# Mixer and MLP of a transformer block project x times the norm's weights, and multiply by the norm's root when the result leaves PSUM

## The reference

```python
x = x + 0.5 * gate * swiglu(h, w2_gu, w2_down)      # end of the first block (not shown: where h comes from)
x = rms_norm(x, g_final)                            # the first block's output

def second_block(x, mem, ...):
    x = x + token_mixer(rmsnorm(x, norm_mix), w_in, b_in, ...)
    x = x + cross_attention(rmsnorm(x, norm_xattn), rmsnorm(mem, norm_mem), ...)
    x = x + squared_relu_mlp(rmsnorm(x, norm_mlp), w_up, w_down)
    return rmsnorm(x, norm_final)

def rms_norm(x, g):
    return x * lax.rsqrt(jnp.mean(x * x, axis=-1, keepdims=True) + EPS) * g     # EPS = 1e-6

def token_mixer(xn, w_in, b_in, ...):
    proj = xn @ w_in + b_in      # 4 HGRN heads with q, two forget gates, values, output gate;
    ...                          # 4 mLSTM heads with q, k, values, output gate; 16 gate rows
                                 # then the scans over time, a norm per head, and @ w_out

def squared_relu_mlp(xn, w_up, w_down):
    return jnp.square(jax.nn.relu(xn @ w_up)) @ w_down
```

## Time and profile before

| | |
|---|---|
| three runs | 2507.22, 2506.64, 2500.88 us; median 2506.64 us |
| the profiled execution | 2508.08 us, of which the profile's span is 2506.3 us |
| mean granted TensorE clock | 0.961 of full speed |
| busy: TensorE, VectorE, ScalarE, GpSimd | 2257.2, 1281.5, 839.1, 83.3 us |
| from the last down unit to the first unit of the scan mixer | 1377.35 to 1419.92 us of the span |
| from the last cross-attention output unit to the second MLP unit | 2130.97 to 2149.85 us of the span |

### The profile page before, as it was taken

The page is one execution under the profiler, slowest core; times in us unless marked ns, Lnnn a source line. Parts: engine busy times, 40 slices in busy tenths (PEclk is TensorE's granted clock), DMA queues, the critical chain, the costliest instruction groups (busy, mean ns, idle before and its releaser), DMA issues.

```text
span 2506.3 us, 26989 instructions
## 1 busy us (share of the span) xinstructions
PE 2257.2 (90%) x9880; PEld 1770.0 (71%) x9880; DVE 1281.5 (51%) x2080; ACT 839.1 (33%) x1212; POOL 83.3 (3%) x63
## 2 busy tenths in 40 slices
PE   1799999899999999899999699988768699899998
PEld 1588888676677787688888388855437477688886
DVE  7776868645554434433333545545654344534443
ACT  1322222323324423322223534343434333422323
POOL 1000000100000001000001100000000101000001
PEclk9999999999999999999999899988879899999999
DMA  6354545322122232233333111211113212233332
GB/s 234 118 181 154 187 149 177 104 81 67 51 68 84 65 100 88 76 101 93 101 93 98 37 59 51 60 42 34 34 35 101 83 59 70 73 101 99 94 92 75
DMA packets 63315, 229.92 MB, mean 92 GB/s; under 512 B 7024, under 2 KB 7152, under 8 KB 62960
## 3 DMA queue, kind: packets, MB, share of 16 engines
q1 hardware_dynamic: 61344, 220.90, 28.0%
q0 software_dynamic: 720, 5.57, 0.6%
q10 hardware_dynamic: 1152, 2.10, 0.2%
HBM read 226.45 MB, written 2.10 MB: 91 GB/s over the span
## 4 chain that ended last, share of the span: by engine, by line
PE 81%; DVE 11%; ACT 4%; issue 2%; DMA 1%; POOL 1%; SPq 0%; DVEq 0%; ACTq 0%; POOLq 0%
PE bank L1450 22%; PE bank L1452 21%; PE bank L1451 21%; DVE work L876 3%; PE bank L1660 2%; PE bank L1464 2%; PE bank L1466 2%; PE bank L1465 2%; DVE normed L876 1%; PE bank L1552 1%; PE bank L1577 1%; DVE hlo L876 1%; PE bank L1726 1%; DVE work L1366 1%; DMA raw<-w 1%
## 5 line engine op out<-in xcount | busy, mean ns | idle before, releaser
L1450 PE MATMUL bank<-hhi,whi 128*128 128x512 f32 (+1 forms) x1736 | 696.6, 401 | 68.9 <-DVE hlo L876 35.4
L1451 PE MATMUL bank<-hlo,whi 128*128 128x512 f32 (+1 forms) x1736 | 672.8, 388 | 0.0
L1452 PE MATMUL bank<-hhi,wlo 128*128 128x512 f32 (+1 forms) x1736 | 671.8, 387 | 0.0
L867 DVE TENSOR_TENSOR wlo<-raw,whi 128x1024 fp32r<-128x1024 f32 (+1 forms) x353 | 428.7, 1215 | 316.1 <-ACT whi L436 313.5
L436 ACT ACTIVATE whi<-raw 128x1024 fp32r<-128x1024 f32 (+1 forms) x353 | 367.9, 1042 | 433.3 <-PE bank L1452 390.0
L1450 PEld LDWEIGHTS bank<-hhi,whi 128*128 128x128 f32 x1736 | 330.4, 190 | 177.9 <-issue 69.0
L1452 PEld LDWEIGHTS bank<-hhi,wlo 128*128 128x128 f32 x1736 | 330.6, 190 | 68.3 <-issue 1.2
L1451 PEld LDWEIGHTS bank<-hlo,whi 128*128 128x128 f32 x1736 | 332.0, 191 | 64.9 <-issue 5.0
L1450 PE MATMUL bank<-ghi,whi 128*128 128x512 f32 x864 | 340.0, 394 | 6.2 <-DVE wlo L867 5.7
L1451 PE MATMUL bank<-glo,whi 128*128 128x512 f32 x864 | 336.6, 390 | 0.0
L1452 PE MATMUL bank<-ghi,wlo 128*128 128x512 f32 x864 | 336.5, 389 | 0.0
(11 more groups left out here) (193 smaller groups left out, 1830.4 us busy)
## 6 DMA issues: line engine op xcount, KB each, us to landing
raw<-w SPq DMA_DIRECT2D x409, 512.0 KB, 3.6
raw<-w SPq DMA_DIRECT2D x16, 384.0 KB, 3.1
xT<-x_t POOLq DMA_DIRECT2D x1, 2048.0 KB, 10.4
y_t<-xT ACTq DMA_DIRECT2D x8, 256.0 KB, 2.2
work<-mem_t POOLq DMA_DIRECT2D x1, 1024.0 KB, 5.2
con<-constants POOLq DMA_DIRECT2D x1, 960.0 KB, 13.3
work<-level_mask_in POOLq DMA_DIRECT2D x1, 896.0 KB, 18.2
work<-rope POOLq DMA_DIRECT2D x1, 512.0 KB, 15.3
```

What stands on the lines that cost most here:

```text
L867: nc.vector.tensor_tensor(wlo[v % 2][:, 0:kc * P], raw[u % 4][:, 0:kc * P], whi[v % 2][:, 0:kc * P].bitcast(F32), ALU.subtract).then_inc(w ...
L1450: nc.tensor.matmul(dst[0:m, 0:n], wh[:, ws], hi[:, c, :], start=c == 0, stop=False)
L1451: nc.tensor.matmul(dst[0:m, 0:n], wh[:, ws], lo[:, c, :], start=False, stop=False)
L1452: ins = nc.tensor.matmul(dst[0:m, 0:n], wl[:, ws], hi[:, c, :], start=False, stop=c == kc - 1)
```

## The change

Two identities are used. A projection is linear and the root is one number per token, so (x·g·root) @ w = root·((x·g) @ w): `hhi` and `hlo` can be made from x·g before the root is known, and the root is multiplied in when the bank is evacuated. And the mixer norm of the final norm's output is, but for an epsilon, x·g_final·g_mix over the root mean of (x·g_final)²; its mean of squares with the final norm's root inside is a sum over x²·(g_final² + EPS), so both roots come from the same x.

1. **Final and mixer norm** (`N_FINAL`, `N_MIX2`): during the last eight down units of the second FFN, ScalarE makes `hhi` = x·`fin_mix[0]` (g_final·g_mix) of a finished chunk (`scaled_hi`) before its square, VectorE makes `hlo` (`scaled_lo`) and a second, weighted square `fsq` with `fin_mix[1]`; GpSimd adds both kinds. TensorE runs the first 8 rows of the gate unit, both sums (bank 4 for the mixer's root in `rstd`, bank 5 for the final one, kept in `square_sum`), then the other 8 rows. The final norm's own result, x·g_final·root, is written by VectorE one chunk at a time behind the first eight unit evacuations of the HGRN slots (`x_final`).
2. **Scan mixer**: every unit is evacuated by VectorE with a multiplication by `rstd` (`unit_evac`) to its destination; ScalarE then applies bias and function in place from SBUF, counted by `unit_in`. In the HGRN slots the evacuation stands behind the slot's second item, in the mLSTM heads it stands right behind `split_next`. The transposition of the values (`group_turn`, `group_values`) moves behind the next unit, in HGRN slots behind the next slot's first item. In the lead-in the splits go one unit further ahead and the units run unbroken. The roots of the head norms use `square[1]`, since `rstd` stays in use.
3. **MLP**: `scaled_hi`, `scaled_lo` between the cross-attention output units; the first up unit is cut around the norm's sum. VectorE evacuates with max(bank, 0)·root, ScalarE squares.

The core of the diff:

```diff
@@ scalar @@
+            def scaled_hi(n, c):
+                x_ready(act, n, c)
+                scale = fin_mix[:, 0, c:c + 1] if n == N_FINAL else gain_col(n, c)
+                nc.scalar.activation(hhi[:, c, :], xT[:, c, :], ACT.Identity, bias=zero_col[:, 0:1],
+                                     scale=scale).then_inc(h_hi, 1)
...
                         split(v0 + 2 * kc + c + 1)
                         if part == 2 and c > 0:
+                            if f == 1:
+                                scaled_hi(N_FINAL, c - 1)
                             norm_square((N_MIX, N_FINAL)[f], c - 1)
...
-            norm_stats(N_FINAL, DC - 1)
-            norm_stats(N_MIX2)
-            norm_hi(N_MIX2)
+            scaled_hi(N_FINAL, DC - 1)
+            norm_square(N_FINAL, DC - 1)
             split_next(V_GATE)
+            act.wait_ge(fsum_done, 1)
+            nc.scalar.activation(rstd[:], bank[4][:], ACT.Ln, bias=eps2_col[:, 0:1], scale=1.0 / D).then_inc(fr_ln, 1)
+            act.wait_ge(sum_done, N_FINAL + 1)
+            nc.scalar.activation(square_sum[:], bank[5][:], ACT.Ln, ...).then_inc(rstd_ln, 1)
...
+            split_next(V_HG)
...
-                    act.wait_ge(unit_done, v + 1)
...
+                    act.wait_ge(evac[v % 2], v // 2 + 1)
                     if k in (1, 2):
...
+                        nc.scalar.activation(kk, f, ACT.Sigmoid, bias=neg_b_in[:, col:col + 1],
+                                             scale=-1.0).then_inc(sig_done, 1)
+                        nc.scalar.activation(f, f, ACT.Sigmoid, bias=b_in(col)).then_inc(sig_done, 1)
...
+                        dst, func = unit_dst(v), ACT.Identity if k == 3 else ACT.Silu
+                        nc.scalar.activation(dst, dst, func, bias=b_in(col)).then_inc(unit_in, 1)
@@ vector @@
+            def scaled_lo(n, c):
+                scale = fin_mix[:, 0, c:c + 1] if n == N_FINAL else gain_col(n, c)
+                dve.wait_ge(h_hi, H_AT[N_MIX2 if n == N_FINAL else n] + c + 1)
+                stt(hlo[:, c, :], xT[:, c, :], scale, hhi[:, c, :].bitcast(F32), ALU.mult,
+                    ALU.subtract).then_inc(h_ready, 1)
...
                         split(v + c + 1)
+                        if f == 1 and part == 2 and c > 0:
+                            scaled_lo(N_FINAL, c - 1)
                         residual(v + c, c, mod(2 if f == 0 else 8, c))
+                        if f == 1 and part == 2:
+                            dve.wait_ge(evac[(v + c) % 2], (v + c) // 2 + 1)
+                            if c > 2:
+                                dve.wait_ge(fsq_added, c - 2)
+                            stt(fsq_sum if c == 0 else fsq[c % 2], xT[:, c, :], fin_mix[:, 1, c:c + 1], xT[:, c, :],
+                                ALU.mult, ALU.mult).then_inc(fsq_done, 1)
...
-            norm(N_FINAL)
-            norm(N_MIX2)
+            def unit_evac(v):
+                dve.wait_ge(unit_done, v + 1)
...
+                nc.vector.tensor_tensor(unit_dst(v), bank[v % 2][:], rstd[:], ALU.mult).then_inc(evac[v % 2], 1)
+
+            def x_final(c):
+                dve.wait_ge(rstd_done, N_FINAL + 1)
+                stt(xT[:, c, :], xT[:, c, :], gain_col(N_FINAL, c), square_sum[:], ALU.mult,
+                    ALU.mult).then_inc(normed_done, 1)
...
                         if sl == 0 and h > 0:
                             hg_out(h - 1)
+                        unit_evac(v)
+                        if 5 * h + sl < DC:
+                            x_final(5 * h + sl)
...
+                def ml_unit():
+                    v = units.pop(0)
+                    split_next(v)
+                    unit_evac(v)
...
                     if y > 1 and y % 2 == 1 and units:
-                        split_next(units.pop(0))
+                        ml_unit()
...
-                    dve.wait_ge(evac[v % 2], v // 2 + 1 + 8 * i)
-                    dve.wait_ge(op_ready, J_MLP + c - 1 + DC * i)
-                    nc.vector.tensor_tensor(opnd[c % 2][:], gate_in[c % 2][:], gate_in[c % 2][:], ALU.mult).then_inc(op_src, 1)
+                    dve.wait_ge(unit_done, v + 1 + 16 * i)
...
+                    stt(gate_in[c % 2][:], bank[v % 2][:], 0.0, rstd[:], ALU.max, ALU.mult).then_inc(evac[v % 2], 1)
@@ tensor @@
+            gate_rows_of(bank[V_GATE % 2], 0)
+            pe.wait_ge(fsq_added, DC - 2)
+            nc.tensor.matmul(bank[4][:], ones, fsq_sum, start=True, stop=False)
+            pe.wait_ge(fsq_done, DC)
+            nc.tensor.matmul(bank[4][:], ones, fsq[1], start=False, stop=True).then_inc(fsum_done, 1)
             norm_sum(N_FINAL)
-            norm_sum(N_MIX2)
-            unit(V_GATE, H, first=(h_ready, H_AT[N_MIX2]), rows=((bank[V_GATE % 2], 0), (bank[2], 8)))
+            gate_rows_of(bank[2], 8).then_inc(unit_done, 1)
...
             for k in range(5):
-                unit_part(V_HG + k, H, 0, 2)
-                group_turn(V_HG + k - 1)
-                unit_part(V_HG + k, H, 2, DC)
+                unit(V_HG + k, H)
+            group_turn(V_HG + 3)
...
-            mlp(0, (h_ready, H_AT[N_MLP]))
+            unit_part(V_MLP, H, 0, 5, first=(h_ready, H_AT[N_MLP]))
+            norm_sum(N_MLP)
+            unit_part(V_MLP, H, 5, DC, first=(h_ready, H_AT[N_MLP]))
```

More of the change, by code:

```diff
@@ L733, in _ @@
             for k in range(5):
-                split_next(V_HG + k)
+                split_next(V_HG + k + 1)
                 group_values(V_HG + k - 1)
@@ L1274, in _ @@
             for k in range(5):
-                split_next(V_HG + k)
+                if k > 1:
+                    split_next(V_HG + k + 1)
+                    unit_evac(V_HG + k)
             dve.wait_ge(acol_done, 1)
@@ L1433, in _, with unit @@
         def _(pe):
-            def unit(v, src, dv=0, n=S, first=None, rows=None):
+            def unit(v, src, dv=0, n=S, first=None):
                 kc = chunks_of(v)
@@ L1479, in norm_sum @@
             def norm_sum(n):
-                w = width(n)
+                b = bank[5 if n == N_FINAL else 4][:, 0:width(n)]
                 pe.wait_ge(sq_added, (DC - 2) * (n + 1))
-                nc.tensor.matmul(bank[4][:, 0:w], ones, square_sum[:, 0:w], start=True, stop=False)
+                nc.tensor.matmul(b, ones, square_sum[:, 0:width(n)], start=True, stop=False)
                 pe.wait_ge(sq_done, DC * (n + 1))
-                nc.tensor.matmul(bank[4][:, 0:w], ones, square[1][:, 0:w], start=False, stop=True).then_inc(sum_done, 1)
+                nc.tensor.matmul(b, ones, square[1][:, 0:width(n)], start=False, stop=True).then_inc(sum_done, 1)
             def swiglu(f):
@@ L1603, in _, with gate_rows_of @@
             swiglu(1)
+            def gate_rows_of(dst, off):
+                wh, wl = whi[V_GATE % 2], wlo[V_GATE % 2]
+                for c in range(DC):
+                    pe.wait_ge(h_ready, H_AT[N_MIX2] + c + 1)
+                    ws = slice(c * P + off, c * P + off + 8)
+                    nc.tensor.matmul(dst[0:8, :], wh[:, ws], hhi[:, c, :], start=c == 0, stop=False)
+                    nc.tensor.matmul(dst[0:8, :], wh[:, ws], hlo[:, c, :], start=False, stop=False)
+                    ins = nc.tensor.matmul(dst[0:8, :], wl[:, ws], hhi[:, c, :], start=False, stop=c == DC - 1)
+                return ins
+            pe.wait_ge(w_split, V_GATE + 1)
+            pe.wait_ge(evac[V_GATE % 2], V_GATE // 2)
+            gate_rows_of(bank[V_GATE % 2], 0)
[3 more added lines that the diff above has]
+            nc.tensor.matmul(bank[4][:], ones, fsq[1], start=False, stop=True).then_inc(fsum_done, 1)
             norm_sum(N_FINAL)
-            norm_sum(N_MIX2)
-            unit(V_GATE, H, first=(h_ready, H_AT[N_MIX2]), rows=((bank[V_GATE % 2], 0), (bank[2], 8)))
+            gate_rows_of(bank[2], 8).then_inc(unit_done, 1)
             def group_turn(v):
                 if V_HG <= v < V_ML and (v - V_HG) % 5 == 3:
-                    pe.wait_ge(evac[v % 2], v // 2 + 1)
+                    pe.wait_ge(unit_in, v - V_HG + 1)
                     if v > V_HG + 5:
```

219 lines of the change are left out of this document (127 added, 92 removed).

## The result

The changed kernel takes 2473.05 us (median of 4 runs, 2470.73 to 2482.93), against 2506.93 us (2500.88 to 2508.48) of the kernel before beside it: a ratio of 0.9868, 95% interval 0.9845 to 0.9890, 33.9 us less. On another chip it was 0.9851 (0.9828 to 0.9874). The forecast was 2468, the range 2462 to 2480. The profiled execution took 2473.34 us, its span is 2471.5 us.

A forecast was written before the change was run, and what follows sets the result against it. TensorE, busy 2257.2 of 2506.3 us, bounds the kernel; its idle stretches at the norms can go. Terms −28.1 − 11.7 − 0.9 + 0.3 + 1.9 = −38.5 us give 2468 us for the median, range 2462 to 2480.

The forecast's parts named there:

- the forecast's case: Whole kernel: all terms hold as summed, 2468 us, given 0.77 against the rivals.
- The two large terms: Gains at the final and mixer norm, 28.1 us, and at the MLP's norm, 11.7 us.
- Final and mixer norm, 14.4 us: Last down unit to first scan unit: 14.4 us instead of 42.57, without a pause, a gain of 28.1.
- Their cover: Gate unit's second 24 matmuls hide the final and mixer norm's roots; uncovered they would cost about 3 to 5 us.
- Port collision, 0: Last eight down units: GpSimd's adds stall VectorE at no cost, ends 0 and +6.6; rival of full exclusion 2475, chance 0.08.
- MLP norm, −11.7: Last attention-output unit to second MLP unit: 7.2 us instead of 18.88, a gain of 11.7; root's cover thin.
- the switch without a drain: MLP norm's root: ScalarE's table switch takes 1.28 us, not the skill's 2.66 with a drain, which would lose 1 us more.
- Lead-in, −0.9: Five units, gate chain and eight-column turns before the scan: 31.0 us instead of 31.9, bounds −1.7 and +1.5.
- HGRN, +0.3: HGRN heads: added evacuations and x passes fit VectorE's idle time except after a head change; +0.3 us, bounds 0 and +2.
- mLSTM, +1.9: mLSTM heads: evacuation and shaping delay the decays; heads 1 and 2 +0.8 each, head 0 +0.25; bounds −1 and +5.
- the turn's 0.78: mLSTM heads: the 0.78 us wait of the values' turn goes, since it now stands behind the next unit.
- No pause means full clock, so I price all at 0.23: Final norm: gate unit's matmuls of 8 rows run at full clock, 0.23 us start to start.

The follow-up runs named there:

- wsq_twice: The changed kernel with VectorE's weighted square made twice, first result unused, in each of the last eight down units; 2482.29 us, ratio 0.9893.
- exps_first: The changed kernel with the mLSTM heads' first decays and first two exponentials ahead of the first unit's evacuation and shaping; 2469.69 us, ratio 0.9846.
- split_early: exps_first plus the second unit's weight split two decay products earlier and ScalarE's third exponential ahead of the first unit's shaping; 2473.66 us, ratio 0.9853.
- all_moves: The changed kernel with split_early's mLSTM order, turns inside the first scan slot, and VectorE's first two decay products behind the fourth scan unit; 2469.94 us, ratio 0.9840.
- turn_in_slot: The changed kernel with the turn of the first head's values and the eight-column turns moved into the first scan slot; 2477.63 us, ratio 0.9877.

## Why the prediction was right, and where it was off

Forecast −38.5 us, measured −33.9 (a gain of 27.6 to 38.9, from the ratio's interval), the forecast's case and inside its range. By the stages of the two profiles it was −32.6, so the sum was 5.9 us too favourable: 2.3 in the mLSTM heads, 2.3 in a stage that it didn't hold, 1.3 in lead-in and HGRN, all of one sign. The two large terms, 39.8 us together, were right to 0.1, and they carried it.

- **Final and mixer norm, 14.4 us:** 14.45. Full clock, no idle, roots covered. Their cover is worth 2.6 us against 3 to 5 estimated.
- **Port collision, 0:** right for TensorE, and closer than it looked. The estimate of 4.2 us of VectorE per 4.1 us slot was 4.27 and thus sound, but whether such a slot costs nothing hung on slack of which 0.9 us were left; wsq_twice shows what lies behind the edge.
- **MLP norm, −11.7:** 11.7 by the profiles, 11.8 by undoing it alone. The forecast of the switch without a drain held: the exponential starts 0.02 us after the load at 2114.05.
- **Lead-in, −0.9 and HGRN, +0.3:** with the clock up in both, 233.4 against 234.44, −1.0; with it down after the change only, up to +0.7. The lead-in alone is 30.60 against 31.90, −1.3, and the slot behind the first head change pays 0.2 where 0.3 was forecast.
- **mLSTM, +1.9:** the mis-sized term, 4.2 by the two profiles and 3.2 to 4.5 over all that keep this order. Heads 1 and 2 were right (+0.8 each; +0.97 and +0.75 here), by the delay forecast: the third unit of head 1 came 1.96 late for 1.9, though the wait before it, forecast near 1.9, was 1.14 and in head 2 1.37. Head 0 was priced at +0.25 and cost +1.5 to +2.6. Its wait for the last decay product grew from 3.19 to 4.00 in every changed profile, and a wait of 0.5 for low weights replaced the turn's 0.78. The larger part is the clock. Windows of the value sums, the kernel before and then the changed one:

```profile
1691.58:1701.16 9.58, 8.89 (x32) 5.52 (x33) 4.27 (x3) 1.19 (x2) 0.00 (x0) 1.00 0.00 0
```

```profile
1662.80:1674.07 11.27, 10.58 (x33) 6.47 (x33) 4.27 (x3) 1.19 (x2) 0.00 (x0) 0.85 0.00 0
```

The same sums, 8.89 us of work at 1.00 and 10.58 at 0.85: 1.7 us, behind a wait that is 0.8 longer. All three profiles of the kernel before keep 1.00 there; in each of the eleven others the wait is 4.0 and the clock is lower. That the longer wait lets the clock fall is argued from this; no run took the wait away. It can't be the wait alone: in exps_first, split_early and all_moves it is 4.0 as well, but the clock in the sums is 0.77 to 0.78, here exps_first:

```profile
1662.12:1674.28 12.16, 11.47 (x33) 6.83 (x33) 4.28 (x3) 1.19 (x2) 0.00 (x0) 0.78 0.00 0
```

These three reach the sums 0.7 to 1.0 us earlier in the head (36.97 us in exps_first, 38.01 in the changed kernel) and take 0.9 to 1.1 us longer over them, which is why head 0 gained nothing.

- **What the sum did not hold:** +2.3 us in the memory's K projections, in a stage that the change does not touch. "No pause means full clock, so I price all at 0.23" was right at the norm and silent on the stages that pause of themselves.

## What to carry to other kernels

Where a norm's root can be multiplied in behind the projection, the norm needed no pause here: scale the operands by the gain alone, put the sum inside the first unit that uses them, and multiply by the root on evacuation. The work that this moves onto the evacuation was nearly free where TensorE fills its slots (the HGRN heads) and was paid where TensorE already waited (the mLSTM heads), so price it head by head and look for what stands behind a blocking evacuation. Before moving "useless" small work off TensorE, ask whom it was giving time.

## What the runs showed of the hardware

- VectorE's instruction with two SBUF inputs took 1.77 us beside GpSimd's adds and 0.74 alone, and GpSimd's adds 1.60 to 1.75 against the 1.37 of the earlier trace rows, and against 1.26 with VectorE idle in the kernel before:

```profile
1393.96 1.26 POOL L421 TENSOR_TENSOR square_sum<-square_sum,square 128x512 f32<-128x512 f32 x1 [0.49 <-POOL square_sum L421]
```

The weighted square, which reads one tile twice, only went to 1.01. The Trainium skill (GPSIMD Engine Reference, Specifications) names the contention; its size here was 1.0 us on 0.75.
- The code up to the second FFN's sum, unchanged but for three small vector instructions: 1000.9 to 1009.7 us in fourteen profiles, while the 372.7 us of FFN behind it repeat to 0.05 in the thirteen that leave it as it is.
- In turn_in_slot one wait of 2.44 us, in place of one of 0.53, went with a stage 4.3 us longer for the same matmuls. The wait is 1.9 of them; a granted clock of 0.50 over 6 us and more is what else differs.
